# Half of the sparse attention's gate projection moved inside that attention, and bias transfers spread over GpSimd's queue

## The reference

```python
def dsa_mixer(xn, positions, w_in, q_norm, k_norm, w_out):
    q, k, v, z, qi, ki, wi = jnp.split(xn @ w_in, cuts, axis=-1)   # 1024 columns each of q, k, v, z
    q = rope(rmsnorm(q.reshape(bsz, seq, B_HEADS, B_HEAD_DIM), q_norm), positions)
    k = rope(rmsnorm(k.reshape(bsz, seq, B_HEADS, B_HEAD_DIM), k_norm), positions)
...
    # per block of 128 queries: index scores, the best 128 keys of those visible, softmax over them
    score = jnp.einsum("qh,qhs->qs", w_b, relu(jnp.einsum("qhd,sd->qhs", qi_b, ki_b)))
    top_val, top_idx = lax.top_k(score, topk)
...
    return (o * jax.nn.silu(z)) @ w_out

bias = rpb[:, dr_idx][:, :, dc_idx]        # neighbourhood attention, 8 heads
```

## Time and profile before

| what | us |
|---|---|
| median of 3 runs | 3179.75 (3177.03 to 3197.86) |
| profiled execution: span, the only time given for it | 3181.7 |
| PE busy | 3088.6 (97%) |
| weight loads of PE (PEld) busy | 2023.0 (64%) |
| DVE / ACT / POOL busy | 1655.3 / 943.4 / 1499.5 |
| first convolution and its output projection, about | 24 to 247 |
| index projection / gate of b / index scores | 254 to 297 / 297 to 341 / 342 to 365 |
| q, k, v of b / sparse attention / its output projection | 365 to 497 / 503 to 604 / 605 to 650 |

### The profile page before, as it was taken

How to read it: one execution, slowest core, us unless ns; L and a number is a source line. 1 busy time by engine, 2 the same in 40 slices (tenths; PEclk the granted TensorE clock), 3 DMA queues, 4 the chain that set the end, 5 groups by cost and what they waited for, 6 DMA issues and landing times.

```text
span 3181.7 us, 40196 instructions
## 1 busy us (share of the span) xinstructions
PE 3088.6 (97%) x15516; PEld 2023.0 (64%) x15516; DVE 1655.3 (52%) x3302; ACT 943.4 (30%) x1464; POOL 1499.5 (47%) x788
## 2 busy tenths in 40 slices
PE   7999998998999999998999999999999999999998
PEld 6888785687677877886777444565655444444444
DVE  6333597548544441017424997444443365556664
ACT  2001225423741011115123223343433222222222
POOL 4664469755035674566556344333333333333331
PEclk9998999999999999999999999999999999999999
DMA  4222122123332222222223433454444755665551
GB/s 143 106 80 108 55 106 51 43 82 115 116 117 106 106 100 106 93 80 74 80 106 140 162 149 137 167 198 181 188 198 188 252 194 198 211 211 205 198 193 63
DMA packets 139831, 429.99 MB, mean 135 GB/s; under 512 B 8640, under 2 KB 79424, under 8 KB 116544
## 3 DMA queue, kind: packets, MB, share of 16 engines
q1 hardware_dynamic: 125216, 353.40, 31.2%
q10 hardware_dynamic: 7200, 68.68, 5.2%
q0 software_dynamic: 7296, 6.31, 0.8%
HBM read 358.10 MB, written 73.40 MB: 136 GB/s over the span
## 4 chain that ended last, share of the span: by engine, by line
PE 87%; DVE 9%; ACT 1%; issue 1%; DMA 1%; POOL 0%; SPq 0%; ACTq 0%; DVEq 0%; POOLq 0%
PE bank L1087 14%; PE bank L1088 14%; PE bank L1089 14%; PE bank L1110 4%; PE bank L653 4%; PE bank L648 4%; PE bank L649 4%; PE bank L681 3%; PE bank L676 3%; PE bank L907 3%; PE bank L677 3%; PE bank L902 3%; PE bank L903 3%; PE bank L777 2%; DVE hF L1731 1%; PE bank L785 1%
## 5 line engine op out<-in xcount | busy, mean ns | idle before, releaser
L2413 POOL TENSOR_TENSOR work<-ring,work 128x4096 bf16<-128x4096 f32 x64 | 530.8, 8293 | 894.5 <-ACT work L1532 894.5
L1087 PE MATMUL bank<-work 128*128 128x512 bf16 x2048 | 776.9, 379 | 3.4 <-DVE work L2251 2.7
L1088 PE MATMUL bank<-work 128*128 128x512 bf16 x2048 | 776.9, 379 | 0.0
L1089 PE MATMUL bank<-work 128*128 128x512 bf16 x2048 | 776.7, 379 | 0.0
L2437 POOL CAST w_parts<-ring 128x1024 fp32r<-128x1024 f32 (+3 forms) x212 | 233.9, 1103 | 653.5 <-DMA ring<-in_wstream 158.9
L2439 POOL TENSOR_TENSOR w_parts<-ring,w_parts 128x1024 fp32r<-128x1024 f32 (+3 forms) x212 | 514.7, 2428 | 17.0
L2251 DVE TENSOR_TENSOR work<-hF,work 128x512 bf16<-128x512 f32 x128 | 307.8, 2405 | 253.1 <-ACT work L1616 250.0
L1089 PEld LDWEIGHTS bank<-work 128*128 128x128 bf16 x2048 | 200.5, 98 | 242.1 <-issue 0.8
L1087 PEld LDWEIGHTS bank<-work 128*128 128x128 bf16 x2048 | 200.7, 98 | 238.3 <-issue 4.0
L1088 PEld LDWEIGHTS bank<-work 128*128 128x128 bf16 x2048 | 200.5, 98 | 234.8 <-issue 0.6
L1532 ACT ACTIVATE work<-ring 128x4096 bf16<-128x4096 f32 x64 | 231.5, 3617 | 209.4 <-PE bank L1089 180.0
(11 more groups left out here) (341 smaller groups left out, 4928.5 us busy)
## 6 DMA issues: line engine op xcount, KB each, us to landing
ring<-in_wstream SPq DMA_DIRECT2D x128, 2048.0 KB, 7.7
hidden<-hF ACTq DMA_DIRECT2D x32, 1024.0 KB, 3.9
gates<-work ACTq DMA_DIRECT2D x16, 2048.0 KB, 8.3
hF<-hidden SPq DMA_DIRECT2D x32, 1024.0 KB, 6.7
work<-gates SPq DMA_DIRECT2D x32, 1024.0 KB, 10.2
rpb_tiles<-in_rpb POOLq DMA_DIRECT2D x192, 16.0 KB, 2.4
work<-rpb_tiles POOLq DMA_DIRECT2D x24, 128.0 KB, 4.5
ring<-in_wstream SPq DMA_DIRECT2D x5, 512.0 KB, 4.0
```

The lines of the kernel that those rows point to most:

```text
L1087: pe.matmul(out, a(0), b(0), start=(start and k == 0), stop=False)
L1088: pe.matmul(out, a(0), b(1), start=False, stop=False)
L1089: mm = pe.matmul(out, a(1), b(0), start=False, stop=(stop and k == n - 1))
L2413: nc.gpsimd.tensor_tensor(SPLIT[:, p, 1, :], ring[:, p, :], SPLIT[:, p, 0, :], ALU.subtract).then_inc(lo, 1)
```

## The change

1. The gate's second half (4 chunks) leaves the place ahead of the index scores. Its slot is loaded as the last of b_in's, its chunks get the last numbers (`LATE_Z`), and TensorE runs its matmuls five at a time at the ends of the attention's steps: chunk i in steps 7 i to 7 i + 4, into bank 6. In step 7 i + 5 ScalarE takes tanh(z / 2), in 7 i + 6 VectorE makes (tanh + 1) x z; `finish` of pairs 4 to 7 multiplies by that and by 0.5.
2. Gated heads are written in the place of the queries (`B_QK`) instead of `hF`. `rest`, an operand of the late matmuls, is overwritten only behind them: the rests of pairs 0 to 5 are made in steps 28 to 31.
3. The 192 bias transfers are spread: 9 behind each of the slots 1 to 7 of a_in0, 36 behind each of the late gate's chunks 1 to 3, 21 behind b_out's second chunk.
4. The reloads of the last stage count on one semaphore for each half instead of two.

```diff
+LATE_Z = CHUNK["b_in"] + 28
+LATE_STEPS = 7
...
+load_after(("b_in", 1), ("b_in", 7))
...
+            def tiled(self, x):
+                return x.rearrange("p (t c) -> p t c", t=NT) if self.tag == "b" else x
+            def o(self, k):
+                return B_QK[:, :, k * P:(k + 1) * P] if self.tag == "b" else hF[:, k, :]
...
# TensorE
+            def late_gate(s):
+                i, r = s // LATE_STEPS, s % LATE_STEPS
+                if not (0 <= i < 4 and r < 5):
+                    return
+                c = LATE_Z + i
+                w = chunk_parts(c, KT, P)
+                if r == 0:
+                    pe.wait_ge(signal("parts_made"), c + 1)
+                    if i:
+                        pe.wait_ge(signal("b_z_gated"), i)
+                terms = [(l, 0, k) for k in range(KT) for l in range(2)] + [(0, 1, k) for k in range(KT)]
+                for n in range(5 * r, min(5 * r + 5, len(terms))):
+                    l, x, k = terms[n]
+                    mm = pe.matmul(bank[:, 6, :], w[l][:, k, :], (b_rounded, rest)[x][:, k, :],
+                                   start=(n == 0), stop=(n == len(terms) - 1))
+                if r == 4:
+                    mm.then_inc(signal("parts_used"), 1)
...
                     modulate(s)
+                    if fill:
+                        fill(s)
...
-            project_features("b_in", CHUNK["b_in"], FIRST["b_in"], b_rounded, rest)
+            project_features("b_in", CHUNK["b_in"], FIRST["b_in"], b_rounded, rest, halves=range(1))
             index_scores()
...
-            attention(b_att)
+            attention(b_att, fill=late_gate)
# ScalarE
+                def late_tanh(i):
+                    act.wait_ge(signal("parts_used"), LATE_Z + i + 1)
+                    act.activation(B_Z[:, 4 + i, :], bank[:, 6, :], ACT.Tanh, scale=0.5)\
+                        .then_inc(signal("b_z_by_act"), 1)
...
                     for w in a.units_at(s):
                         move_qk(w)
+                    if a.tag == "b" and s >= 0 and s % LATE_STEPS == 5 and s // LATE_STEPS < 4:
+                        late_tanh(s // LATE_STEPS)
...
-            take_gate("b_in", "b_in", B_Z, [(j, j) for j in range(8)])
+            take_gate("b_in", "b_in", B_Z, [(j, j) for j in range(4)])
# VectorE
                     dve.wait_ge(summed, NT * w + NT)
-                    v.tensor_tensor(hF[:, w, :], bank[:, 7, :], a.z[:, w, :], ALU.mult).then_inc(o_taken, 1)
+                    if a.tag == "b" and w >= 4:
+                        dve.wait_ge(signal("b_z_gated"), w - 3)
+                        v.scalar_tensor_tensor(out=a.o(w), in0=a.tiled(bank[:, 7, :]), scalar=0.5,
+                                               in1=a.tiled(a.z[:, w, :]), op0=ALU.mult, op1=ALU.mult)
...
+                def late_gate(i):
+                    dve.wait_ge(signal("b_z_by_act"), i + 1)
+                    v.scalar_tensor_tensor(out=B_Z[:, 4 + i, :], in0=B_Z[:, 4 + i, :], scalar=1.0, in1=bank[:, 6, :],
+                                           op0=ALU.add, op1=ALU.mult).then_inc(signal("b_z_gated"), 1)
+                rests_at = {4 * (k + 2): [k] for k in range(6)}
+                if a.tag == "b":
+                    rests_at = {28: [0, 1], 29: [2], 30: [3, 4], 31: [5]}
...
-                    if s % NT == 0 and w >= 2:
-                        rest_o(w - 2)
+                    for k in rests_at.get(s, ()):
+                        rest_o(k)
+                    if a.tag == "b" and s >= 0 and s % LATE_STEPS == 6 and s // LATE_STEPS < 4:
+                        late_gate(s // LATE_STEPS)
# GpSimd
+            places = [(v, r, h) for v in range(3) for r in range(8) for h in range(NA_HEADS)]
+            def arrange_bias(first, last):
+                for v, r, h in places[first:last]:
...
                         g.tensor_tensor(parts[1], source, parts[0], ALU.subtract).then_inc(made, 1)
                         c += 1
+                        if between:
+                            between(m, at)
                     pool.wait_ge(made, c)
                     pool.sem_inc(slot_used[n % 2], 1)
+            def beside_conv(m, at):
+                if m and at == 3:
+                    arrange_bias(9 * m - 9, 9 * m)
+            def beside_sparse(m, at):
+                if at:
+                    arrange_bias(63 + 36 * at - 36, 63 + 36 * at)
+            def behind_sparse(m, at):
+                if m == 0 and at == 1:
+                    arrange_bias(171, 192)
-            weight_parts("a_in0", 8, KT, 512)
+            weight_parts("a_in0", 8, KT, 512, between=beside_conv)
...
-            weight_parts("b_in", 2, KT, 512)
-            weight_parts("b_in", 6, KT, 512, 2, 2, 8)
-            arrange_bias()
-            weight_parts("b_out", 2, KT, 512)
+            weight_parts("b_in", 1, KT, 512)
+            weight_parts("b_in", 6, KT, 512, 2, 2, 4)
+            weight_parts("b_in", 1, KT, 512, 0, 1, 28, between=beside_sparse)
+            weight_parts("b_out", 2, KT, 512, between=behind_sparse)
```

More of the change, by code:

```diff
@@ L660, in conv_in, with project_features @@
                     body(i)
-            def project_features(name, c0, n0, hi, lo, opening=None, free=(), between=None):
+            def project_features(name, c0, n0, hi, lo, opening=None, free=(), between=None, halves=range(2)):
                 made, used = signal("parts_made"), signal("parts_used")
-                for m in range(2):
+                for m in halves:
                     if m < len(free):
@@ L722, in project_b @@
             def project_b(i):
[L724 removed]
+                ready, by_act, c0 = signal("b_in_ready"), signal("b_in_by_act"), CHUNK["b_in"] + 4
                 for p in range(2):
[L726 removed]
+                    pe.wait_ge(by_act, max(4, 8 * i + 4 * p - 8))
                     for q in range(4):
@@ L1340, in take_b @@
                         else:
-                            act.wait_ge(signal("parts_used"), CHUNK["b_in"] + 8 * i + 4 * p + 4)
+                            act.wait_ge(signal("parts_used"), CHUNK["b_in"] + 8 * i + 4 * p)
                         act.activation(dst[:, t, ds(column + p * 512, 512)], bank[:, 4 * p + t, :], ACT.Copy)\
@@ L2241, in outputs @@
                 w_made, w_hi, w_lo = (signal(x) for x in ("w_made", "w_hi_made", "w_lo_made"))
-                gates_in, hidden_in = ([signal(x + str(p)) for p in range(2)] for x in ("gates_in", "hidden_in"))
+                reloaded = [signal("reloaded0"), signal("reloaded1")]
                 def body(i):
                     for p in range(2):
-                        dve.wait_ge(gates_in[p], 16 * i + 16)
-                        dve.wait_ge(hidden_in[p], 16 * i + 16)
+                        dve.wait_ge(reloaded[p], 32 * i + 32)
                         def lower(j):
@@ L2358, in _ @@
             pool.wait_ge(signal("constants_in"), 48)
-            def arrange_bias():
-                for v in range(3):
+            places = [(v, r, h) for v in range(3) for r in range(8) for h in range(NA_HEADS)]
+            def arrange_bias(first, last):
+                for v, r, h in places[first:last]:
                     qc, kc = (0, 16, 48)[v], (0, 8, 32)[v]
-                    for r in range(8):
-                        for h in range(NA_HEADS):
-                            near = rpb_d[h, qc:qc + 16, (7 - r) * 64:(15 - r) * 64].rearrange(
-                                "p (k c) -> p k c", c=64)[:, :, kc:kc + 32]
-                            pool.dma_start(rpb_tiles[h, v, 16 * r:16 * r + 16, :].rearrange("p (k c) -> p k c", c=32),
-                                          near).then_inc(signal("n_rpb_arranged"), 16)
+                    near = rpb_d[h, qc:qc + 16, (7 - r) * 64:(15 - r) * 64].rearrange(
+                        "p (k c) -> p k c", c=64)[:, :, kc:kc + 32]
+                    pool.dma_start(rpb_tiles[h, v, 16 * r:16 * r + 16, :].rearrange("p (k c) -> p k c", c=32),
+                                   near).then_inc(signal("n_rpb_arranged"), 16)
             def load_bias(h):
@@ L2416, in split_lo, with weight_parts @@
                         pool.sem_inc(slot_used[p], 1)
-            def weight_parts(name, slots, k_tiles, width, tokens=0, m0=0, c0=0, chunk=None, per=P):
+            def weight_parts(name, slots, k_tiles, width, tokens=0, m0=0, c0=0, chunk=None, per=P, between=None):
                 made, hi, used = signal("parts_made"), signal("parts_hi"), signal("parts_used")
```

26 lines of the change are left out of this document (14 added, 12 removed).

## The result

The median after is 3195.28 us (13 runs, 3189.44 to 3200.29), that of the kernel before on the same chips 3181.20 (13 runs, 3176.27 to 3198.18). The ratio is 1.0037 with a 95% interval of 1.0024 to 1.0049, so some 12 us slower (7.6 to 15.6); the medians lie 14.1 apart. 3194.4 was forecast.

What follows compares the result with a forecast made beforehand. TensorE was taken to bound the kernel. Convolution +11.9, earlier index scores -16.2, sparse attention +18.9 and the rest 0 gave +14.6 us on 3179.75, so 3194.4 us; the 8 in 10 range was 3177 to 3211.

Steps and rivals of the forecast that it cites:

- convolution: First convolution: nine bias transfers between GpSimd's splits make TensorE wait 1.7 us, seven times; +11.9 us, between 10.9 and 16.
- earlier start and the splits beside the rotations: Ahead of the sparse attention: index scores start 22.1 us earlier, two splits slow VectorE's rotations by 5.9; -16.2 us.
- attention: Sparse attention: moved matmuls, less hidden work and a cleaner end, plus rests, splits and late gates; +18.9 us, +12 to +25.
- nine and the gap take 0.6 + 4.8 = 5.4 us: First convolution: nine transfers and the gap ahead of them delay GpSimd's next split, so it starts 3.5 us late.
- The bound of -14: Bound for the earlier index scores: -14 us if the longer wait at the meeting (6.1 + 5.9 us) also costs clock.
- Hidden: Sparse attention: gaps take part of the late matmuls, 1.5 times the idle per group as in the latent attention; -6.0 us.
- The end: Sparse attention, last score product to b_out: both b_out chunks split earlier, so 14.0 becomes 10.3 us; -3.7.
- Late rests: Sparse attention, steps 28 to 31: six subtractions, 4.1 us, where VectorE has room for perhaps 2.6; +1.5 us.
- Splits in the attention: Sparse attention: four GpSimd splits, each right behind a filled stretch, cost +1.0 each; +4.0 us, from 0 to 8.
- The gate doesn't hide: Denies a rival: gate hides in attention's waits, filled group under about 11.6 us, attention -2.2; 3173 us, chance 0.12.
- The transfers hold GpSimd: Denies a rival: transfers don't hold GpSimd or find slack, so the convolution costs nothing; +2.7, 3182 us, chance 0.13.
- The clock didn't fall: Rival: clock falls at each new wait, seven in the convolution, four in the attention, 17.6 us more; 3212 us, chance 0.11.

Runs made afterwards that it cites:

- after_late_split: The changed kernel, with GpSimd waiting for the end of the meeting before the sparse attention before it splits the late gate's first chunk; 3188.86 us, ratio 1.0017.
- before_split_first: The kernel before, with b_out's first two chunks split ahead of the 192 bias transfers instead of behind them; 3182.78 us, ratio 1.0001.
- combined: The changed kernel, convolution transfers three at a time, late gate's first split held behind the meeting, b_out's second behind the attention; 3174.54 us, ratio 0.9978.
- after_b_out_late: The changed kernel, with GpSimd waiting for the end of the attention before splitting b_out's second chunk, the 21 transfers ahead of that wait; 3188.75 us, ratio 1.0024.
- before_clean: The kernel before, 63 transfers three at a time in the convolution, b_out's first split held behind the meeting, its second behind the attention; 3177.67 us, ratio 0.9985.
- combined_sync: The changed kernel, late gate's first split held behind the meeting, b_out's second behind the attention, all 192 transfers issued by SyncE; 3176.25 us, ratio 0.9981.
- before_conv9: The kernel before, with 63 of its 192 bias transfers nine behind the fourth chunk of each of a_in0's slots 1 to 7; 3194.31 us, ratio 1.0035.

## Why the prediction was right

| term | forecast | measured |
|---|---|---|
| convolution | +11.9 | +9.3 |
| earlier start and the splits beside the rotations | -16.2 | -16.3 |
| attention | +18.9 | +20.2 |
| output projection of b | 0 | -0.5 |
| sum | +14.6 | +12.7; ratio +11.8, medians +14.1 |

The half us of the output projection is the clock's: in the kernel before `b_out` began at half clock. The total is closer than its parts deserve: the convolution was 2.6 too dear and the attention 1.3 too cheap, and within the attention terms missed in both directions. That the medians lie 14.1 apart for a forecast of 14.6 is luck on top of it; the ratio of the runs gives 11.8 and the trace 12.7.

**The convolution** was 2.6 us too dear. The pace held (0.51 to 0.54 us each) and the clock stayed. The step that was off is "nine and the gap take 0.6 + 4.8 = 5.4 us": here no gap of 0.6 stood ahead, 4.2 us over seven groups. A gap of 1.0 costs 1.32, so the price was not simply the idle time, and that gave some 2 back.

**The meeting** was right in sum and mechanism: 22.1 earlier, 5.9 given back. I had counted two splits beside rotations; one of the two met the four small operations instead, and cost the same. That the price is the splits' is shown by after_late_split (5.9 back, less 1.6 of clock in another stage), by before_split_first (5.7 more without the change) and by combined (22.2 in place of 16.3). The bound of -14, for clock lost to the longer wait, was not needed: the half clock behind the meeting was as long before.

**The attention** was 1.3 too cheap, of terms that miss in both directions:
- Hidden: 3.5 us rather than 6.0. The filled group above holds 19 of the late products (105 matmuls for 86), 4.29 us of work at 0.2256 each, and grew by 3.59: 0.7 hidden, and 96 products make 5.05 such groups. The step that was off is "1.5 times the idle": what was hidden is the group's idle time of before, 0.72, and no more. This is worked out, not isolated by a run.
- The end: 10.0 in place of 14.0, -4.0 for a forecast of -3.7 and +1.5. Two clean splits are worth more than I said, 5.3 (before_split_first, where the end took 8.7).
- Late rests: +1.5 forecast. Moving four of them changed nothing, but the end with all six took 10.0 where before_split_first has 8.7, so up to 1.3 may be theirs or the clock's, and no run took them out.
- Splits in the attention: +4.0 forecast; waits of 0.79, 0.76, none and 2.83 are 4.4. The sum holds and the step behind it doesn't: "each right behind a filled stretch" gave each 1.0. The last one, behind the last products of step 25, came where no products follow, among the scalings of the last turns, and cost 3.5 with the half clock behind it (after_b_out_late).
- What is left, 20.2 - (22.1 - 3.5 - 4.0 + 4.4) = 1.2, is the late gates' share and the clock's; no run parted them. The forecast had +1.0 for the gates and nothing for the clock. But from the last products of the first late chunk to the first of the second there pass 10.8 us in the kernel after, where 0.50 was granted from 525 to 528, and 9.6 in combined, where the clock stayed at 1.00: some 1.2 us, an estimate, may be the clock's.

**The rivals.** The gate doesn't hide: 14.61 us for a filled group, the bound was 11.6. The transfers hold GpSimd. The clock didn't fall at the convolution's gaps of 1.0 us (granted 1.00 over the whole stage), but did in the attention, behind 0.95 + 1.88 and behind the single 0.79, though not behind the same 0.79 in combined: this rival had a small part, which the forecast put at nothing. One table load, so tanh shares the one of exp here.

The Trainium skill, "SBUF — State Buffer", section "SBUF: two separate sides", has GpSimd's transfers starve while VectorE runs a two-port operation. That does not show here either: nine take 4.68 to 4.92 us, 0.52 to 0.55 each, in a stage where VectorE works 98 of 238 us; no row says which of its operations are of that kind. What slows is VectorE, beside GpSimd's arithmetic.

## What to carry to other kernels

When one engine's work stretches another's (here VectorE's rotations, from 1.37 to 4.23 us beside one split), an early piece of work isn't free because its own engine is idle: hold it until the other's critical chain is over, and place it where nobody waits. Transfers go between pieces of work in portions no longer than the slack there (three here, 1.6 us), or onto a queue that does nothing else. Products moved into a stage whose bound engine is already busy nine tenths fill only what is idle there, here some 2 of 22 us.

## What the hardware showed that I had not expected

- GpSimd stood still for some 3 us after the 113th bias transfer wherever it issued them, whatever lay between: at 551 us before, at 531 after (rows of POOL with 3.05 us of "issue" idle), 3.95 us in before_clean behind 63 + 50. It is so in all eleven kernels that have GpSimd issue them, and I have no cause for it. In the kernel after TensorE did not wait for it; in combined it lies in the run of transfers that made the late split above 1 us later.

```profile
533.80 6.34 POOL L2424 DMA_DIRECT2D rpb_tiles<-in_rpb  x12 [3.05 <-issue]
```

- The granted clock fell to half with PE busy throughout, in the index projection's last chunks, whose matmuls are 72 wide: in combined_sync 1.00 until 282 us, then

```profile
282.00:286.00 4.00, 4.00 (x27) 0.66 0.98 395
286.00:290.00 4.00, 4.00 (x20) 0.50 0.29 44
```

  Where it began differed from one execution to another by a few us, and with it the stage: from its first product to the gate's first pass 39.1 us here, 40.8 in combined, 41.8 in before_conv9.
- The first product started at 22.6 to 23.1 us in six of the fourteen profiled executions and at 24.6 to 25.1 in eight, whatever had been edited. A span's difference of 2 us between two profiled executions says nothing here.
